# Decay factors of a gated delta rule: clipping and difference on ScalarE, GpSimd multiplying by 0/1 masks

## What is computed

```
g_cum = cumsum(g) within chunks of 64 tokens          # g <= 0, so g_cum never rises
decay = exp(where(causal, g_cum[i] - g_cum[j], -inf))  # [64, 64] per head and chunk
# used three times: in the strictly lower matrix of k k^T (times beta) that is inverted,
# in its transpose, and in the causal q k^T
o = norm(scan over chunks of the state with these matrices) * silu(z)
```

## Time and profile before

| what | value |
|---|---|
| median of 3 runs | 3846.2 us (3845.32 to 3846.3) |
| the profiled execution's own time | 3846.3 us |
| its span in the profile | 3844.5 us |
| TensorE busy | 3712.6 us, 97% of the span |
| VectorE busy | 2914.0 us, 76% |
| ScalarE busy | 1883.9 us, 49% |
| GpSimd busy | 176.6 us, 5% (184 instructions) |
| chain that ended last | TensorE 74%, VectorE 13%, issue 6%, ScalarE 4%, DMA 2% |
| mean granted TensorE clock | 0.994 |

### The profile page before, as it was taken

The page is one execution under the profiler, slowest core; times in us unless marked ns, Lnnn a source line. Parts: engine busy times, 40 slices in busy tenths (PEclk is TensorE's granted clock), DMA queues, the critical chain, the costliest instruction groups (busy, mean ns, idle before and its releaser), DMA issues.

```text
span 3844.5 us, 67090 instructions
## 1 busy us (share of the span) xinstructions
PE 3712.6 (97%) x25590; PEld 3398.1 (88%) x25590; DVE 2914.0 (76%) x4028; ACT 1883.9 (49%) x2810; POOL 176.6 (5%) x184
## 2 busy tenths in 40 slices
PE   1999999999999999999999999999999999999998
PEld 1999999888888999999988888998987899989988
DVE  8788887878889778888696886666676666666676
ACT  1556565435544455565534554454665434444365
POOL 0111111000000012121000000000000000000000
PEclk8999999999999999999999999999999999999999
DMA  9544443864478844434486444545534555555543
GB/s 392 181 152 147 142 147 137 305 240 168 152 251 327 278 150 145 149 137 152 153 322 210 163 159 175 186 167 180 191 118 149 187 186 184 183 184 185 185 150 124
DMA packets 138691, 720.35 MB, mean 187 GB/s; under 512 B 37696, under 2 KB 38144, under 8 KB 62336
## 3 DMA queue, kind: packets, MB, share of 16 engines
q1 hardware_dynamic: 111456, 631.31, 45.8%
q10 hardware_dynamic: 27040, 86.32, 6.6%
HBM read 711.22 MB, written 2.16 MB: 186 GB/s over the span
## 4 chain that ended last, share of the span: by engine, by line
PE 74%; DVE 13%; issue 6%; ACT 4%; DMA 2%; DVEq 1%; ACTq 0%; SPq 0%
PE bank L303 27%; PE bank L304 13%; PE bank L284 6%; PE bank L285 6%; PE bank L286 6%; DVE Wl L368 4%; PE bank L2438 2%; PE bank L2437 2%; PE bank L2436 2%; DMA raw<-in_ada 1%; ACT Wh L362 1%; DVE gm_more L1321 1%; PE bank L326 1%; PE bank L330 1%; PE bank L1083 1%
## 5 line engine op out<-in xcount | busy, mean ns | idle before, releaser
L362 ACT CAST Wh<-raw 128x1024 fp32r<-128x1024 f32 x1124 | 1171.7, 1048 | 1600.6 <-PE bank L304 681.0
L368 DVE TENSOR_TENSOR Wl<-raw,Wh 128x1024 fp32r<-128x1024 f32 x1124 | 1380.1, 1232 | 658.9 <-ACT Wh L362 655.4
L303 PE MATMUL bank<-H,Wh 128*128 128x512 f32 x3744 | 1334.1, 400 | 4.8 <-DVE WS L355 4.6
L304 PE MATMUL bank<-H,Wl 128*128 128x256 f32 x3744 | 1049.5, 280 | 0.0
L284 PE MATMUL bank<-H,Wh 128*128 128x256 f32 x3296 | 973.1, 295 | 2.0 <-DVE Wl L368 1.2
L285 PE MATMUL bank<-H,Wh 128*128 128x256 f32 x3296 | 931.6, 283 | 0.0
L286 PE MATMUL bank<-H,Wl 128*128 128x256 f32 x3296 | 931.2, 283 | 0.0
L303 PEld LDWEIGHTS bank<-H,Wh 128*128 128x128 f32 x3744 | 703.1, 188 | 181.5 <-issue 9.3
L304 PEld LDWEIGHTS bank<-H,Wl 128*128 128x128 f32 x3744 | 706.9, 189 | 0.2
L284 PEld LDWEIGHTS bank<-H,Wh 128*128 128x128 f32 x3296 | 629.4, 191 | 16.4 <-issue 5.7
L285 PEld LDWEIGHTS bank<-H,Wh 128*128 128x128 f32 x3296 | 629.5, 191 | 7.9 <-issue 4.8
(11 more groups left out here) (411 smaller groups left out, 4187.7 us busy)
## 6 DMA issues: line engine op xcount, KB each, us to landing
raw<-in_stream SPq DMA_DIRECT2D x560, 1024.0 KB, 4.8
WS<-in_ada ACTq DMA_DIRECT2D x94, 512.0 KB, 6.1
raw<-in_ada SPq DMA_DIRECT2D x32, 1024.0 KB, 7.5
gm_more<-in_ada ACTq DMA_DIRECT2D x20, 512.0 KB, 7.3
WS<-rows_d ACTq DMA_DIRECT2D x16, 512.0 KB, 5.0
KR<-in_ada ACTq DMA_DIRECT2D x14, 512.0 KB, 7.2
raw<-in_stream SPq DMA_DIRECT2D x8, 512.0 KB, 6.9
gm_more<-WS ACTq DMA_DIRECT2D x32, 128.0 KB, 4.9
```

The source lines that it names most:

```text
L303: pe.matmul(out[:, :], wh, x[:, kt, :, :], start=kt == 0, stop=False)
L304: mm = pe.matmul(out[:, 0:T], wl, x[:, kt, 0, :], start=False, stop=kt == KT - 1)
L362: act.copy(Wh[:, n % 4, :], raw[:, (sbk + 2) % 4, k * (D // 2):(k + 1) * (D // 2)]).then_inc(hi_ready, 1)
L368: dve.tensor_tensor(Wl[:, n % 4, :], raw[:, (sbk + 2) % 4, k * (D // 2):(k + 1) * (D // 2)], Wh[:, n % 4, :].bitcast(F32), ALU.subtract).t ...
```

## The change

ScalarE now makes the differences. `activation(..., Relu, scale, bias)` over one unit (128x128) gives max(0, scale * row + bias), the row being the broadcast log of the columns and the bias the unit's own log decay on the partition, one column. The clipping keeps what is outside the mask finite, so that `Exp` with scale -1 gives at most 1 everywhere and the masks can be zeros and ones. The masks are made so in the setup. GpSimd copies the eight bias columns to `unit_log` (a multiplication by one), fills "odd", and multiplies each factor by its mask after the `Exp`.

```diff
+        unit_log = SEC_X[:, 24:32].rearrange("p (a u) -> p a u", a=2)
...
-            S.done(dve.tensor_scalar(const("m_low"), const("pair"), -BIG, BIG, ALU.mult, ALU.add), "dve", "m_pair")
-            S.done(dve.tensor_scalar(const("m_up"), above, -1.0, None, ALU.mult), "dve", "m_up")
-            S.done(dve.scalar_tensor_tensor(const("m_upd"), ident, -BIG, above, ALU.mult, ALU.subtract), "dve", "m_upd")
+            S.done(dve.tensor_copy(const("m_low"), const("pair")), "dve", "m_pair")
+            S.done(dve.tensor_scalar(const("m_up"), above, 1.0 / BIG, 1.0, ALU.mult, ALU.add), "dve", "m_up")
+            S.wait(dve, "dve", "m_up")
+            S.done(dve.tensor_tensor(const("m_upd"), ident, const("m_up"), ALU.add), "dve", "m_upd")
...
-            S.done(act.copy(TOK[:, 0:2, :].rearrange("p a (h t) -> p a t h", t=2), B[2][:, 0:64].rearrange("p (a t h) -> p a t h", t=2, h=HEADS)), "act", "tok_log")
+            for a, sign in ((0, 1.0), (1, -1.0)):
+                S.done(act.activation(TOK[:, a, :].rearrange("p (h t) -> p t h", t=2), B[2][:, 32 * a:32 * a + 32].rearrange("p (t h) -> p t h", t=2),
+                                      ACT.Copy, scale=sign), "act", f"tok_log{a}")
...
+            def fall(e):
+
+                rows = gb[:, e % 2].rearrange("p h (t c) -> p (h t) c", c=P)
+                for u in range(4):
+                    F.done(act.activation(u4(E[:, e, :])[:, u, :], rows[:, u, :], ACT.Relu, scale=-1.0 if e else 1.0,
+                                          bias=unit_log[:, 0 if e else 1, u:u + 1]), "act", f"fall{e}_{u}")
+
             def front(n):
...
+                if n == (7 if chain else 5):
+                    F.wait(act, "dma", "gb", f)
+                    F.wait(act, "pool", "log", f)
+                    fall(0)
+                if n == (9 if chain else 6):
+                    if chain:
+                        S.wait(act, "pe", "Z64", r)
+                    fall(1)
+                    F.wait(act, "act", "fall1_3", f)
+                    F.done(act.activation(E[:, 0:2, :], E[:, 0:2, :], ACT.Exp, scale=-1.0), "act", "decay")
...
-                    F.wait(act, "pool", "E2", f)
-                    F.done(act.activation(E[:, :, :], E[:, :, :], ACT.Exp, scale=-1.0), "act", "decay")
                 if n == (SCAN + 6 if chain else SCAN + 5):
                     F.wait(act, "dve", "conv5_3", f)
                     F.done(act.activation(tv, cs[:, 4:6, :], ACT.Tanh, scale=0.5), "act", "tanh_v")
+                    fall(2)
+                    F.wait(act, "act", "fall2_3", f)
+                    F.done(act.activation(E[:, 2, :], E[:, 2, :], ACT.Exp, scale=-1.0), "act", "decay2")
...
-                F.wait(pool, "dma", "gb", f)
-                pause()
-                rows = [gb[:, 0].rearrange("p h (t c) -> p (h t) c", c=P), gb[:, 1].rearrange("p h (t c) -> p (h t) c", c=P)]
+                if chain:
+                    F.wait(pool, "act", "decay2", r)
+                F.done(pool.tensor_tensor(unit_log, TOK[:, 0:2, bass.ds(i * 4, 4)], ones[:, 0:8].rearrange("p (a u) -> p a u", a=2), ALU.mult), "pool", "log")
                 e = [u4(E[:, n, :]) for n in range(3)]
-                for n, (a, b, m) in enumerate(((rows[0], tok(1, i), "m_low"), (tok(0, i), rows[1], "m_up"), (tok(0, i), rows[0], "m_upd"))):
-                    if chain and n == 1:
-                        S.wait(pool, "pe", "Z64", r)
-                        pause()
+                if chain:
+                    S.wait(pool, "pe", "turn64", r)
+                    pause(8)
+                F.done(pool.tensor_tensor(even(Mm[:], 1), even(mask4("ident"), 1), even(mask4("ident"), 1), ALU.mult), "pool", "odd")
+                F.wait(pool, "act", "decay", f)
+                pause(9)
+                for n, m in enumerate(("m_low", "m_up", "m_upd")):
                     if n == 2:
-                        if chain:
-                            S.wait(pool, "pe", "turn64", r)
-                            pause(8)
-                        F.done(pool.tensor_tensor(even(Mm[:], 1), even(mask4("ident"), 1), even(mask4("ident"), 1), ALU.mult), "pool", "odd")
-                    if chain and n == 2:
-                        S.wait(pool, "pe", "o_second", r)
-                        pause()
-                    F.done(pool.tensor_tensor(e[n], a, b, ALU.subtract), "pool", f"e{n}")
-                    F.wait(pool, "pool", f"e{n}", f)
-                    F.done(pool.tensor_tensor(e[n], e[n], mask4(m), ALU.add), "pool", f"E{n}")
+                        F.wait(pool, "act", "decay2", f)
+                        pause(10)
+                    F.done(pool.tensor_tensor(e[n], e[n], mask4(m), ALU.mult), "pool", f"E{n}")
...
-                    F.wait(dve, "act", "decay", r)
+                    F.wait(dve, "pool", "E1", r)
...
                     S.wait(dve, "pe", "qk", r)
+                    F.wait(dve, "pool", "E2", r)
```

## The result

The changed kernel takes **3891.2 us** (median of 4 runs, 3889.84 to 3894.04) where the kernel before takes 3846.0 in the same session (3845.32 to 3846.3). The ratio is 1.0117, 95% interval 1.0105 to 1.0128: slower, by three times the predicted 14.6 us and outside the range. The profiled execution took 3894.04 us, span 3892.2, mean granted clock 0.989; against the 3846.3 of before that is 47.7 us to explain (it is the slowest of the four; by the medians the loss is 45.2). Of the executions reported further down, one each of e1_vn_first, e5_spin, f1_e2_step8 and of the kernel before was far slower, at a mean granted clock of 0.47 to 0.81, and is left out of every median and ratio.

A forecast was written before the change was run, and what follows sets the result against it. TensorE was taken to bound the kernel, busy 61.93 of 62.00 us in a chained pass. The terms summed to 14 x (0.97 + 0.15) - 1.1 = +14.6 us, so 3846.3 + 14.6 = 3860.9 us; range 3845 to 3871.

The forecast's parts named there:

- E0 and E1 beside the third tap: Step 9, chained passes: E0's multiplication on GpSimd blocks the third tap, so "vn" and TensorE are late; +0.97 us per pass.
- bound of 2.3: Upper bound in us on the lateness at "vn" in step 9, if both multiplications get ahead of the third tap.
- E2 at step 14: Step 14: added ScalarE and GpSimd work makes `t_of2` some 0.7 us later against slack 0.64; +0.15 us per pass.
- Nothing for ScalarE, "log", "odd" and the removed contention: ScalarE's work at steps 7 and 9, "log", "odd" and VectorE's shortened operations at 279 to 285 us: worth 0.
- First pass: First pass of each layer, 2 in all: fewer GpSimd operations remove TensorE's wait for the squares; -1.1 us.
- The tap did not get in first: Rival at step 9: the third tap goes ahead of E0's multiplication, nothing lost at "vn"; about 3847.3 us; chance 0.32.
- the second rival: Step 9: E0 gets in before the second tap, E1 before the third; another 1.3 us per pass, about 3879; chance 0.06.
- A gain from GpSimd's shorter work: Rival: six large GpSimd operations per pass become three, VectorE gets some 2 us back; at most 4.9 us, 3841.4; chance 0.05.

The follow-up runs named there:

- e1_vn_first: Changed kernel with "vn" issued on VectorE ahead of the three taps of step 9 instead of behind them: 3852.70 us, ratio 1.0017.
- e5_spin: Changed kernel with four unused matmuls of constants on TensorE ahead of its wait for "vn": 3886.50 us, ratio 1.0099.
- f1_e2_step8: Changed kernel with "vn" ahead of the taps and ScalarE's part of E2 moved from step 14 to step 8: 3869.04 us, ratio 1.0056.
- e3: Changed kernel with GpSimd waiting for its own first mask multiplication before it issues the second: 3870.27 us, ratio 1.0057.
- h1: Kernel before with two GpSimd multiplications by ones added near the taps of step 9, no added ScalarE work: 3875.76 us, ratio 1.0073.
- f2: Changed kernel with "vn" ahead of the taps, all differences and Exp by step 8, E2's multiplication behind `o_second`: 3850.94 us, ratio 1.0008.
- f3: Changed kernel, "vn" at its old place, E0 and E1 two steps earlier, E2's multiplication behind the second square: 3851.27 us, ratio 1.0007.
- the repeat: Changed kernel run and profiled once more, unaltered: median 3888.58 us, ratio 1.0112; its profiled execution took 3882.8.
- e4b: Changed kernel with GpSimd waiting for "vn" before it multiplies E0 and E1, chained passes only: 3857.80 us, ratio 1.0026.
- h2: Kernel before with h1's two multiplications and a third of 128x256 behind them, after a wait on the first: 3880.73 us, ratio 1.0082.
- h3: Kernel before with h1's two multiplications and "odd" moved from before them to right behind, with no wait: 3876.34 us, ratio 1.0073.

## Why the prediction was wrong

**E0 and E1 beside the third tap: right place, wrong size. This is the step that failed.** Up to the collision it held: TensorE bound, no slack at "vn", the four differences in 1.28 us, so (1.28 - 0.39)/3 = 0.30 from one to the next, and the `Exp` ending 3.32 us behind the start of the cast of step 8. In the time of before, where that cast starts at 290.00, this is 293.32 against the forecast 293.3, and the first multiplication starts at 293.68. The step then said that it "holds until 294.85" and that the third tap "ends 0.3 us after GpSimd lets go". It let the tap in between the two multiplications. In the changed kernel there is no "between": GpSimd goes from one to the other without a gap, and the tap waits through both, +2.1 instead of +0.97. e3 puts the gap in and gets 0.8 to 0.9. The prediction held the ends: its bound of 2.3 was nearly reached. But it gave that case 0.06, because it knew only one way to it (E0 ahead of the second tap). For the gap in its main term it gave no reason; the nearest is in that rival, where "the one who waits is served at the next gap". The trace of the kernel before would have spoken for it. In the first pass of a layer, GpSimd goes from a mask addition to "odd" with no wait between, beside the first of the taps of the earlier trace rows:

```profile
162.55 1.48 DVE L1321 SCALAR_TENSOR_TENSOR gm_more<-Y,PAR,gm_more 128x256 f32<-128x256 f32 x1
...
162.44 1.30 POOL L1299 TENSOR_TENSOR WS<-WS,C 128x512 f32<-128x512 f32 x1
163.70 0.80 POOL L1293 TENSOR_TENSOR WS<-C 128x256 f32<-128x256 f32 x1
```

The tap was let in there, and "odd" took 0.80 instead of 0.60. So the kernel before had a row for being let in with no wait between, and that row did not mean that VectorE always gets in.

**The clock: not foreseen.** No term, bound or rival held it. It is 7 x 1.47 = 10.3 us in the profiled run, as much as the range had above the forecast. The prediction costed a TensorE wait at its length.

**E2 at step 14: right mechanism, half the size.** `t_of2` (326.05 to 327.12 in the changed kernel) ends at 321.60 in the time of before, against 321.5, and the weight half beside E2's multiplication takes 1.60 us instead of 1.22. The term that was too small is the wait that follows from it: 0.33 us at the matmul of L1087 against +0.15. The cast of step 14 starts at 319.53, which is 314.01 in the time of before, against 313.85.

**Nothing for ScalarE, "log", "odd" and the removed contention: right.** ScalarE's casts start behind its new work with no wait of TensorE, and h1 makes most of the loss without that work. VectorE got back some 2 us per pass of stretched operations at steps 6 and 7 and this bought nothing.

**First pass: right.** TensorE is busy 60.94 of 61.00 instead of 60.44, and the wait for the squares has no row any more.

**The rivals.** The tap did not get in first. The arrangement of the second rival, E0 ahead of the second tap, appeared only in the first chained pass; in the other 13 its cost came by the way that no rival had. A gain from GpSimd's shorter work did not appear: f2 and f3, which avoid most of the harm, end at no difference. The upper end of the range, 3871, would have held e3 and f1; by the bound of 2.3 for "vn" with the other terms the prediction itself could have written 3846.3 + 14 x 2.45 - 1.1 = 3879.5, and the repeat with two low passes took 3882.8.

The Trainium skill, SBUF — State Buffer, "Who interferes with whom", has the one that issues first hold the port for the whole instruction. For the first multiplication the trace agrees: it started at 296.92, 0.13 us ahead of the tap, and held it back. For the second it does not: that started at 298.17, after the tap, and still went first in 13 of 14 passes. In e3 and in one pass of the repeat the tap went ahead of it, as the rule would have it.

## What to carry to other kernels

When two or more GpSimd operations stand in a row, cost what VectorE has in front of them at their *sum*, not at the first one, unless something separates them; the sum was 2.1 us here, the single 0.8 to 0.9. If two VectorE operations stand before the hand-over, being let in between saves little: the wait was still 1.7 us (h1). Look where VectorE hands over to TensorE without slack, and keep GpSimd's row of work away from there: what is stretched elsewhere cost a quarter of it (e4b) or too little for the times to tell from nothing (f2, f3). And an idle time of TensorE can cost more than its length: watch the granted clock in the stretch behind it.

## What the hardware did that I had not expected

- One VectorE operation of 0.48 us took 2.66, through two GpSimd operations of 1.28 us, though it had started before the second of them. In the same program it was let in between them in one pass of 14, and GpSimd's pair then took 2.70 instead of 2.50.
- With the pair beginning one tap earlier (h1) the waiting tap was let in between in all 14 passes, in e1 in six of eight; and a third GpSimd operation (h2, h3) never kept VectorE out.
- Starting first did not secure the turn: in e4b a VectorE operation that started 0.04 to 0.09 us before the pair was held through both in all 14 passes (3.66 to 3.72 us for 1.22).
- After a wait of 2.0 to 2.2 us the granted clock fell to 0.50 within 1.6 us, for about 3 us, in 7 passes of 14 in one run, in 2 of 13 in another; after waits of 1.7 us (h1, h2, h3) in none. With matmuls of constants in the wait (e5) it never fell. Each fall cost 1.3 to 1.6 us.
